# Latent attention: the next two heads' query and key products placed between the attention units of the present pair, values first

## The chip, the cores and the metric

The kernel runs on one core of a Trainium2 chip. The metric is the time of one execution on the device in microseconds; the time before is the median of three runs. One execution was also recorded by the hardware profiler, and all rows below come from it.

## What is computed

The program is a stack of two transformer models of width 1024 on 512 tokens, all in fp32. The change touches one step of the second model, the latent attention (16 heads, query and key of 64 + 32 components, values of 64). Cut to what matters:

```python
def _mla_mixer(h, w_in, q_norm, w_uq, kv_norm, w_ukv, w_out):
    cq, ckv, k_rope = jnp.split(h @ w_in, [MLA_Q_RANK, MLA_Q_RANK + MLA_KV_RANK], axis=-1)
    q = (_rmsnorm(cq, q_norm) @ w_uq).reshape(B, S, H, MLA_NOPE + MLA_ROPE)
    kv = (_rmsnorm(ckv, kv_norm) @ w_ukv).reshape(B, S, H, MLA_NOPE + MLA_V)
    q = jnp.concatenate([q[..., :MLA_NOPE], _apply_rope(q[..., MLA_NOPE:], cos, sin)], axis=-1)
    k_rope = jnp.broadcast_to(_apply_rope(k_rope[:, :, None, :], cos, sin), (B, S, H, MLA_ROPE))
    k = jnp.concatenate([kv[..., :MLA_NOPE], k_rope], axis=-1)
    v = kv[..., MLA_NOPE:]
    o = _dense_causal_attention(q * (MLA_NOPE + MLA_ROPE) ** -0.5, k, v)
    return o @ w_out
```

The causal attention takes a softmax over the keys up to each query. The ranks are 384 for the queries and 256 for keys and values.

## The kernel before

Activations lie with features on the partitions and the 512 tokens along the free axis, as blocks of 128 x 512. Each engine has its own program, in order; they meet through semaphores. TensorE's products go in turn into four PSUM banks (`pbank`, counter `m`), its small results (scores, transposes, rope turns, attention outputs) in turn into four others (`sbank`, counter `s`). `product()` and `small()` on TensorE wait until the result four places earlier in the same sequence was taken out; `full`/`sfull` wait for a result, `took`/`stook` say that its bank is free. The table `STAGES` (lines 69 to 74 for this step) fixes how many products, small results and weight blocks each stage has. The sync engine streams the weights through a ring of three tiles of 16 blocks of 128 x 128 (`stream()`, line 589 issues the loads); a tile is loaded again once TensorE has gone past it.

An fp32 product of 512 columns is two MATMUL rows of the trace. The stages of the latent attention are:

- `mla_in` (line 1022): six input products, ScalarE's copies and squares, VectorE's reciprocals (line 2072) and normed blocks (line 2075; `mla_normed` counts five, three for the queries, then two for keys and values), the rope of the one shared key part (lines 2080 to 2083), which GpSimd then copies to all 16 heads in one instruction (line 684).
- `mla_q` (line 1034): for each of 16 heads three weight blocks by 512 tokens, and one product later the rope turn, a product with the constant `turn_mla` into a small bank. ScalarE copies the query from its bank, VectorE updates the rope rows in three operations (lines 2090, 2091, 2093).
- `mla_k` (line 1043): eight key weight pairs, two heads each, two matmuls of 64 rows a head.
- `mla_v` (line 1052): values with tokens on the partitions, eight banks of results, copied by VectorE (line 2099).
- `mla` (line 1055): 64 units, `u = 4 * head + n`, where unit n of a head has 128 queries and (n + 1) x 128 keys. TensorE computes the scores of unit u; VectorE scales and masks them (line 2108), reduces the maximum (line 2111) and negates it (line 2112); ScalarE takes the exponential and its sum; VectorE takes the reciprocal (line 2118) and normalises (line 2119), one unit later. TensorE transposes the probabilities three units later (line 1074), ScalarE copies them to the area `B`, and after the fourth unit of a head TensorE forms the output product from all four. VectorE's order is score work of u, then normalisation of u - 1; ScalarE's is exponential of u, then copy of the transposes of u - 2. The order of the small results is written out in `MLA_ORDER`.
- `mla_out`: eight output products, added to the residual by VectorE.

Of the kernel before, what the change touches and what calls it, by code (L numbers as in the profile page):

```python
# [31 lines left out]
def stage(name, products, smalls, blocks):  # L32
    STAGES.append((name, products, smalls, blocks))
# [33 lines left out]
second_ffn(6)  # L67
stage("norm7", 0, 0, 0)
stage("mla_in", 6, 3, 6 * DB)
stage("mla_q", 16, 16, 3 * 16)  # L70
stage("mla_k", 16, 0, 16)
stage("mla_v", 8, 0, 16)
stage("mla", 0, 16 * 9, 0)
stage("mla_out", DB, 0, DB * DB)
second_ffn(8)
second_ffn(9)
# [42 lines left out]
def stream():  # L119


    tiles, place, skipped, plain = [], {}, 0, None
    for name, _, _, blocks in STAGES:
        w, n = AT[name][2], int("".join(c for c in name if c.isdigit()) or -1)
        if name == f"up{n}" and n in QUARTERED:
            for p in range(QUARTERED[n]):
                tiles.append(((name, p), [(0, TILE, w + skipped + TILE * p)]))
            plain = None
        elif name == f"down{n}" and n in QUARTERED:
            ff = QUARTERED[n]  # L130
            for q in range(DB // 2):
                for c, (k, nk) in enumerate(chunks(ff)):
                    tiles.append(((name, len(chunks(ff)) * q + c),
                                  [(8 * e, nk, w + skipped + (2 * q + e) * ff + k) for e in range(2)]))
            plain = None
        else:
            order = range(blocks)
            if name == "rw_in":
                order = [b for first, n_blocks in RW_PARTS.values() for b in range(first, first + n_blocks)]
            for b in order:  # L140
                if plain is None or plain == TILE:
                    tiles.append((None, []))
                    plain = 0
                place[w + b] = (len(tiles) - 1, plain)
                at, of = w + b + skipped, tiles[-1][1]
                if name in ("up1", "down1", "up4", "down4"):
                    i = b + (2 * FF1 * DB if name.startswith("down") else 0)
                    at = AT[f"up{n}"][2] + skipped + 48 * (i // 24) + i % 24
                if of and of[-1][2] + of[-1][1] == at:
                    of[-1] = (of[-1][0], of[-1][1] + 1, of[-1][2])  # L150
                else:
                    of.append((plain, 1, at))
                plain += 1
            if name in ("down1", "down4"):
                skipped += FFN_BLOCKS
    return tiles, place
# [124 lines left out]
def build(nc, io):  # L281
    with ExitStack() as ctx:
# [167 lines left out]

        MLA_ORDER = {}
        MLAG = 3
        for u in range(16 * NB + MLAG):
            if u < 16 * NB:
                MLA_ORDER["scores", u] = len(MLA_ORDER)
            if u >= MLAG:
                MLA_ORDER["turned", u - MLAG] = len(MLA_ORDER)
                if (u - MLAG) % NB == NB - 1:
                    MLA_ORDER["output", (u - MLAG) // NB] = len(MLA_ORDER)

        def mla_small(what, u):
            return AT["mla"][1] + MLA_ORDER[what, u]
# [255 lines left out]
        def _(pe):  # L718
# [312 lines left out]
            s = small()  # L1031
            done(pe, AT["mla_in"][0] + 5)
            mm(sbank(s)[:, :], const("turn_mla"), B[:, 21, :], True, True, small_full)
            begin("mla_q")
            for j in range(17):
                if j < 16:
                    project(lambda k: B[:, 16 + k, :], 3,
                            (lambda k: pe.wait_ge(S("mla_normed"), k + 1)) if j == 0 else settled, cols=96)
                if j >= 1:
                    s = small()  # L1040
                    done(pe, AT["mla_q"][0] + j - 1)
                    mm(sbank(s)[0:96, :], const("turn_mla")[0:96, 0:96], A[0:96, j - 1, :], True, True, small_full)
            begin("mla_k")
            pe.wait_ge(S("mla_normed"), 5)
            for j in range(8):
                w = weight(2)
                for e in range(2):
                    m = product()
                    for k in range(2):
                        mm(pbank(m)[0:64, :], w[:, k * P + 64 * e:k * P + 64 * e + 64], B[:, 19 + k, :], k == 0, k == 1,  # L1050
                           product_full if k == 1 else None)
            begin("mla_v")
            for half in range(2):
                token_major(lambda k: B[:, 19 + k, :], 2, T, settled)
            begin("mla")
            pe.wait_ge(S("mla_q_ready"), 16)
            pe.wait_ge(S("mla_keys_spread"), 1)
            for j in range(4):
                done(pe, AT["mla_k"][0] + 12 + j)
            for j in range(4):  # L1060
                done(pe, AT["mla_v"][0] + 4 + j)
            for u in range(16 * NB + MLAG):
                if u < 16 * NB:
                    hd, n = u // NB, u % NB
                    s = small()
                    mm(sbank(s)[:, 0:(n + 1) * P], A[0:96, hd, n * P:(n + 1) * P], B[0:96, hd, 0:(n + 1) * P], True, True,
                       small_full)
                if u >= MLAG:
                    v = u - MLAG
                    hd, n = v // NB, v % NB  # L1070
# [5 lines left out]
                    if n == NB - 1:  # L1076
                        o = small()
                        for j in range(NB):
                            sdone(pe, mla_small("turned", v - 3 + j))
                        rows = slice(64 * (hd % 2), 64 * (hd % 2) + 64)  # L1080
                        for b in range(NB):
                            mm(sbank(o)[rows, b * P:], A[:, 16 + 2 * b + hd // 8, hd % 8 * 64:hd % 8 * 64 + 64],
                               B[:, 16 + 4 * (hd % 2) + b, b * P:], b == 0, b == NB - 1,
                               small_full if b == NB - 1 else None)
            begin("mla_out")
            sdone(pe, mla_small("output", 14))
            sdone(pe, mla_small("output", 15))
# [239 lines left out]
        def _(act):  # L1327
# [210 lines left out]
            for j, width in ((0, 384), (1, 256)):  # L1538
                sfull(act, s0 + j)
                stook(a(TM[:, j, :], sbank(s0 + j)[:, :], ACT.Sqrt, scale=1 / width, bias=vec("eps", 0)), s0 + j)  # L1540
            m0 = AT["mla_q"][0]
            for j in range(16):
                full(act, m0 + j)
                took(a(A[0:96, j, :], pbank(m0 + j)[0:96, :], ACT.Identity), m0 + j)
            m0 = AT["mla_k"][0]
            for j in range(16):
                full(act, m0 + j)
                took(a(B[0:64, j, :], pbank(m0 + j)[0:64, :], ACT.Identity), m0 + j)
            for u in range(16 * NB + MLAG - 1):
                if u < 16 * NB:  # L1550
                    n, o = u % NB, u % 4
                    act.wait_ge(S("mla_minus_max"), u + 1)
                    p = TM[:, o, 0:(n + 1) * P]
                    a(p, p, ACT.Exp, bias=SM[:, o:o + 1], accum_out=SM[:, 4 + o:5 + o]).then_inc(S("mla_exp"), 1)
                if u < MLAG - 1:
                    continue
                v = u - MLAG + 1
# [2 lines left out]
                sfull(act, s)  # L1560
                if v >= 8 and n == 0:
                    sfull(act, mla_small("output", hd - 2))
                stook(a(B[:, 16 + 4 * (hd % 2):17 + 4 * (hd % 2) + n, n * P:(n + 1) * P],
                        sbank(s)[:, 0:(n + 1) * P].rearrange("p (b t) -> p b t", t=P), ACT.Identity), s)
                if n == NB - 1:
                    s = mla_small("output", hd)
# [123 lines left out]
        def _(dve):  # L1690
# [390 lines left out]
            own(tt(kr, kr, cos, ALU.mult))  # L2081
            sdone(dve, s0 + 2)
            tt(kr, kr, TM[64:96, 2, :], ALU.add).then_inc(S("mla_key"), 1)
            s0 = AT["mla_q"][1]
            for j in range(16):
                q, t = A[64:96, j, :], TM[64:96, 2 + j % 2, :]
                sfull(dve, s0 + j)
                if j == 0:
                    dve.wait_ge(S("mla_key"), 1)
                stook(tt(t, sbank(s0 + j)[64:96, :], sin, ALU.mult), s0 + j)  # L2090
                own(tt(q, q, cos, ALU.mult))
                sdone(dve, s0 + j)
                tt(q, q, t, ALU.add).then_inc(S("mla_q_ready"), 1)
            m0 = AT["mla_v"][0]
            for half in range(2):
                for t in range(NB):
                    m = m0 + 4 * half + t
                    full(dve, m)
                    took(dve.tensor_copy(A[:, 16 + 2 * t + half, :], pbank(m)[:, :]), m)
            scale = float(96 ** -0.5)  # L2100
            for u in range(16 * NB + 1):
                if u < 16 * NB:
# [10 lines left out]
                if u >= 1:  # L2113
# [3 lines left out]
                    dve.wait_ge(S("mla_exp"), v + 1)  # L2117
                    own(dve.reciprocal(SM[:, 8 + o:9 + o], SM[:, 4 + o:5 + o]))
                    ts(w, w, SM[:, 8 + o:9 + o], None, ALU.mult).then_inc(S("mla_probs"), 1)
            add_gated("mla_out", 1)  # L2120
            norm2(8, 2)
            up_silu(8)
# [352 lines left out]
```

## Time and profile before

| what | value |
|---|---|
| median of three runs | 4630.73 us (4629.33 to 4631.75) |
| the profiled execution | 4628.95 us, span 4627.1 us |
| TensorE busy | 4311.6 us, 93% |
| VectorE, ScalarE, GpSimd busy | 34%, 14%, 36% |
| TensorE's mean granted clock | 0.956 of full speed |
| the attention units, 2523 to 2693.3 us | 170 us |

A busy share is the time in which an engine executed instructions over the span; a TensorE that is busy may still run at half of its clock. Times in the timeline are microseconds from the span's start, then the duration; in square brackets stands the idle time before an instruction and what ended it.

### The profile page before, as it was taken

How to read it: one execution, taken by the hardware profiler on the slowest of the kernel's cores; microseconds unless marked ns; L12 is line 12 of the kernel's file. 1: busy time of each engine (PE TensorE's matmuls, PEld its weight loads, DVE VectorE, ACT ScalarE, POOL GpSimd, SP SyncE). 2: the span in 40 equal slices, each digit the busy share in tenths (PEclk: the TensorE clock that was granted, in tenths of full speed). 3: DMA queues.
4: the chain of work that ended last, by engine and by line, in shares of the span. 5: the costliest groups of instructions: out<-in, count | busy, mean ns of one | idle time of the engine just before them, and what ended most of it. 6: DMA issues, size and time to landing. Idle time of an engine off the chain costs nothing.

```text
span 4627.1 us, 40198 instructions
## 1 busy us (share of the span) xinstructions
PE 4311.6 (93%) x15784; PEld 2713.2 (59%) x15784; DVE 1581.5 (34%) x2889; ACT 663.2 (14%) x1407; POOL 1663.6 (36%) x1520
## 2 busy tenths in 40 slices
PE   7948999999999999899999789999999889989998
PEld 3323444433644444388853338887888336836887
DVE  3062111026721110333225533323331754453432
ACT  1131000012610000100012410001000231211000
POOL 0003888800048886044410004443443015003442
PEclk9969999999899999999999889999999889989999
DMA  3102434311034342122221012222222123112222
GB/s 120 64 0 109 154 141 155 114 70 55 10 132 155 141 154 104 55 85 89 84 67 45 0 46 86 88 85 74 88 87 86 46 84 92 36 37 73 82 87 68
DMA packets 124346, 387.39 MB, mean 84 GB/s; under 512 B 37568, under 2 KB 40640, under 8 KB 110080
## 3 DMA queue, kind: packets, MB, share of 16 engines
q1 hardware_dynamic: 108848, 302.56, 19.5%
q0 software_dynamic: 15312, 82.27, 4.7%
q8 instruction: 126, 2.06, 0.2%
q14 instruction: 60, 0.49, 0.0%
HBM read 376.39 MB, written 8.39 MB: 83 GB/s over the span
## 4 chain that ended last, share of the span: by engine, by line
PE 89%; DVE 7%; ACT 2%; issue 1%; DMA 1%; POOL 0%; DVEq 0%; ACTq 0%; POOLq 0%
PE bank L722 89%; DVE rstd L1711 1%; DVE normed L1713 1%; ACT temporary L1331 1%; DVE temporary L2323 1%; DVE small_columns L2111 1%; DVE temporary L2108 0%; DMA constant_matrices<-in_constants_dram 0%; ACT area_b L1331 0%; ACT L1331 0%; PE bank L993 0%; DVE normed L1716 0%; DVE temporary L1855 0%; DVE area_b L1818 0%; ACT squares L1331 0%
## 5 line engine op out<-in xcount | busy, mean ns | idle before, releaser
L722 PE MATMUL bank<-normed,weight_ring 128*128 128x512 f32 (+2 forms) x4080 | 1514.1, 528 | 77.0 <-DVE normed L1716 36.1
L722 PEld LDWEIGHTS bank<-normed,weight_ring 128*128 128x128 f32 (+1 forms) x4080 | 781.5, 193 | 766.3 <-issue 689.9
L722 PE MATMUL bank<-area_a,weight_ring 128*128 128x512 f32 (+1 forms) x1776 | 634.9, 514 | 15.3 <-issue 15.3
L722 PEld LDWEIGHTS bank<-area_a,weight_ring 128*128 128x128 f32 x1776 | 339.2, 192 | 288.1 <-issue 267.6
L672 POOL TENSOR_TENSOR area_b<-weight_ring 128x512 f32<-128x512 f32 (+1 forms) x68 | 84.1, 1236 | 1171.7 <-issue 563.1
L722 PE MATMUL bank<-area_b,weight_ring 128*128 128x256 f32 (+3 forms) x1616 | 497.3, 455 | 5.9 <-issue 2.8
L642 POOL TENSOR_SCALAR area_b<-area_b,small_columns 128x384 f32<-128x384 f32 x336 | 418.9, 1247 | 0.0
L722 PEld LDWEIGHTS bank<-area_b,weight_ring 128*128 128x128 f32 (+2 forms) x1616 | 302.2, 187 | 176.7 <-issue 145.4
L644 POOL TENSOR_TENSOR area_b<-area_b 128x384 f32<-128x384 f32 x336 | 335.4, 998 | 28.0
L722 PE MATMUL bank<-area_b 128*128 128x256 f32 (+2 forms) x1200 | 259.7, 379 | 16.2 <-ACT area_d L1331 16.2
L722 PEld LDWEIGHTS bank<-area_b 128*128 128x128 f32 (+1 forms) x1200 | 215.8, 197 | 51.9 <-ACT area_d L1331 16.9
L672 POOL TENSOR_TENSOR area_d<-weight_ring 128x512 f32<-128x512 f32 (+1 forms) x68 | 84.1, 1236 | 449.8 <-PE bank L722 424.4
L722 PE MATMUL bank<-area_b,area_d 128*128 128x256 f32 x1056 | 239.0, 379 | 0.0
L722 PEld LDWEIGHTS bank<-area_b,area_d 128*128 128x128 f32 x1056 | 200.6, 190 | 27.3
L722 PE MATMUL bank<-squares,constant_matrices 128*128 128x512 f32 x282 | 146.1, 645 | 68.4 <-ACT squares L1331 46.2
L722 PE MATMUL bank<-area_b,area_a 128*64 128x128 f32 (+11 forms) x640 | 166.9, 414 | 40.0 <-ACT area_b L1331 22.9
L722 PE MATMUL bank<-normed,area_d 128*128 128x256 f32 (+2 forms) x1088 | 197.9, 339 | 0.2 <-issue 0.2
L1331 ACT ACTIVATE area_d<-area_d 128x512 f32<-128x512 f32 (+1 forms) x104 | 57.7, 563 | 920.9 <-DVE area_d L2012 920.9
L2032 DVE SCALAR_TENSOR_TENSOR residual<-temporary,modulations,residual 128x256 f32<-128x256 f32 x64 | 41.4, 646 | 379.3 <-ACT temporary L1331 378.1
L722 PEld LDWEIGHTS bank<-normed,area_d 128*128 128x128 f32 (+2 forms) x1088 | 156.3, 171 | 24.4 <-issue 2.9
L1331 ACT ACTIVATE temporary<-bank 128x256 f32<-128x256 f32 (+1 forms) x136 | 58.9, 433 | 774.1 <-PE bank L722 774.1
L1746 DVE TENSOR_TENSOR residual<-residual,bank 128x512 f32<-128x512 f32 x32 | 22.0, 688 | 428.6 <-PE bank L722 428.6
(267 smaller groups left out, 4500.7 us busy)
## 6 DMA issues: line engine op xcount, KB each, us to landing
weight_ring<-in_weights_dram SPq DMA_DIRECT2D x377, 512.0 KB, 4.6
weight_ring<-in_weights_dram SPq DMA_DIRECT2D x61, 1024.0 KB, 4.8
area_b<-in_weights_dram POOLq DMA_DIRECT2D x48, 1024.0 KB, 5.2
area_b<-in_weights_dram POOLq DMA_DIRECT2D x48, 512.0 KB, 6.4
weight_ring<-in_weights_dram SPq DMA_DIRECT2D x40, 384.0 KB, 4.4
weight_ring<-in_weights_dram SPq DMA_DIRECT2D x24, 256.0 KB, 3.7
low_scratch<-area_d SPq DMA_DIRECT2D x16, 256.0 KB, 2.0
area_d<-low_scratch SPq DMA_DIRECT2D x16, 256.0 KB, 2.8
```

What stands on the lines that cost most here:

```text
L642: po.tensor_scalar(scaled, part, c, None, ALU.mult).then_inc(S("pool_step"), 1)
L644: i = po.tensor_tensor(total, total, scaled, ALU.add)
L672: po.tensor_tensor(s1, w21, w22, ALU.add).then_inc(S("pool_sum"), 1)
L722: i = pe.matmul(out, lhsT, rhs, start=start, stop=stop)
L1331: return act.activation(out, in_, func, **kw)
L1711: own(dve.reciprocal(RB[:, :], RB[:, :]))
L1713: i = stt(H[:, k, :], X[:, k, :], gain(k), RB[:, :], ALU.mult, ALU.mult)
L1746: took(tt(X[:, k, :], X[:, k, :], pbank(m0 + k)[:, :], ALU.add), m0 + k)
L2032: return stt(x, part, g, x, ALU.mult, ALU.add)
L2111: own(dve.tensor_reduce(SM[:, o:o + 1], w, AX, ALU.max))
L2323: own(dve.reciprocal(r, r))
```

## The change

The stages `mla_q` and `mla_k` are gone. Values come first. Queries, keys and rope turns of heads 0 and 1 follow, and those of each later pair stand between the units of the pair before it: on TensorE the two queries behind the scores of the first two units of a pair, the keys of both behind the third, the two rope turns behind the fifth and sixth. Scores of a head wait for its own query and key. ScalarE takes queries and keys between exponential and transposed copy; VectorE does the rope updates at the ends of its sixth and seventh unit of a pair. The transposed probabilities lie in the area `D` in place of `B`, the rope's scratch in `D` in place of `TM`. The weight blocks are streamed in the new order. The diff, cut:

```diff
-stage("mla_q", 16, 16, 3 * 16)
-stage("mla_k", 16, 0, 16)
-stage("mla_v", 8, 0, 16)
-stage("mla", 0, 16 * 9, 0)
+stage("mla_v", 8, 0, 0)
+stage("mla", 32, 16 * 10, 3 * 16 + 16 + 16)
...
+            if name == "mla":
+
+                order = [*range(64, 80)]
+                for pair in range(8):
+                    order += [*range(6 * pair, 6 * pair + 6), 48 + 2 * pair, 49 + 2 * pair]
...
+        for hd in range(2):
+            MLA_ORDER["rope", hd] = len(MLA_ORDER)
         for u in range(16 * NB + MLAG):
             if u < 16 * NB:
                 MLA_ORDER["scores", u] = len(MLA_ORDER)
+            if u < 14 * NB and u % 8 in (4, 5):
+                MLA_ORDER["rope", u // 8 * 2 + u % 8 - 2] = len(MLA_ORDER)
             if u >= MLAG:
                 MLA_ORDER["turned", u - MLAG] = len(MLA_ORDER)
...
+            def query(hd):
+                at["w"] = w0 + 3 * hd
+                project(lambda k: B[:, 16 + k, :], 3, settled, cols=96)
+
+            def keys(pair):
+                at["w"] = w0 + 48 + 2 * pair
                 w = weight(2)
                 for e in range(2):
                     m = product()
                     for k in range(2):
                         mm(pbank(m)[0:64, :], w[:, k * P + 64 * e:k * P + 64 * e + 64], B[:, 19 + k, :], k == 0, k == 1,
                            product_full if k == 1 else None)
+
+            def rope(hd):
+                s = small()
+                done(pe, mla_query(hd))
+                mm(sbank(s)[0:96, :], const("turn_mla")[0:96, 0:96], A[0:96, hd, :], True, True, small_full)
+
             begin("mla_v")
+            at["w"] = w0 + 64
             for half in range(2):
-                token_major(lambda k: B[:, 19 + k, :], 2, T, settled)
+                token_major(lambda k: B[:, 19 + k, :], 2, T, lambda k: pe.wait_ge(S("mla_normed"), 5) if k == 0 else None)
+            at["w"] = w0
             begin("mla")
-            pe.wait_ge(S("mla_q_ready"), 16)
+            query(0)
+            query(1)
+            keys(0)
+            rope(0)
+            rope(1)
             pe.wait_ge(S("mla_keys_spread"), 1)
...
                     s = small()
+                    if n == 0:
+                        pe.wait_ge(S("mla_q_ready"), hd + 1)
+                        done(pe, mla_key(hd))
                     mm(sbank(s)[:, 0:(n + 1) * P], A[0:96, hd, n * P:(n + 1) * P], B[0:96, hd, 0:(n + 1) * P], True, True,
                        small_full)
+                if u < 14 * NB:
+                    if u % 8 in (0, 1):
+                        query(u // 8 * 2 + 2 + u % 8)
+                    elif u % 8 == 2:
+                        keys(u // 8 + 1)
+                    elif u % 8 in (4, 5):
+                        rope(u // 8 * 2 + u % 8 - 2)
...
                     a(p, p, ACT.Exp, bias=SM[:, o:o + 1], accum_out=SM[:, 4 + o:5 + o]).then_inc(S("mla_exp"), 1)
+                if u < 14 * NB:
+                    hd = u // 8 * 2 + 2
+                    if u % 8 in (1, 2):
+                        query(hd + u % 8 - 1)
+                    elif u % 8 in (3, 4):
+                        key(hd + u % 8 - 3)
...
+            def rope(hd):
+                q, t, s = A[64:96, hd, :], D[64:96, 8 + hd % 2, :], mla_small("rope", hd)
+                sfull(dve, s)
+                stook(tt(t, sbank(s)[64:96, :], sin, ALU.mult), s)
                 own(tt(q, q, cos, ALU.mult))
-                sdone(dve, s0 + j)
+                sdone(dve, s)
                 tt(q, q, t, ALU.add).then_inc(S("mla_q_ready"), 1)
...
+            dve.wait_ge(S("mla_key"), 1)
+            rope(0)
+            rope(1)
...
                     ts(w, w, SM[:, 8 + o:9 + o], None, ALU.mult).then_inc(S("mla_probs"), 1)
+                if u < 14 * NB and u % 8 in (5, 6):
+                    rope(u // 8 * 2 + u % 8 - 3)
```

## Rows read from the trace of the kernel before

**Rows 1.** The page: busy time of each engine, and the chain that ended last

```profile
PE 4311.6 (93%) x15784; PEld 2713.2 (59%) x15784; DVE 1581.5 (34%) x2889; ACT 663.2 (14%) x1407; POOL 1663.6 (36%) x1520
...
PE 89%; DVE 7%; ACT 2%; issue 1%; DMA 1%; POOL 0%; DVEq 0%; ACTq 0%; POOLq 0%
```

**Rows 2.** Busy time by stage, the attention: length; PE, PEld, DVE, ACT, POOL; clock; DMA share; GB/s

```profile
2523.00:2693.30 170.30, 124.94 (x417) 58.40 (x417) 98.16 (x322) 72.93 (x208) 0.00 (x0) 0.85 0.00 1
```

**Rows 3.** The chain of waits ahead of the attention: start, length, what

```profile
2423.65 2.81 issue
2426.46 96.89 PE bank L722 x224
```

**Rows 4.** Timeline of TensorE at the first score and over one head, with ScalarE's last copy

```profile
2524.31 2.40 PE L722 MATMUL bank<-area_b,area_a 96*128 96x128 f32 x8 [0.98 <-DVE area_a L2099]
...
2578.27 3.39 PE L722 MATMUL bank<-area_b,area_a 128*64 128x512 f32 x10 [1.46 <-ACT area_b L1331]
2581.50 0.27 PE L1074 MATMUL bank<-constant_matrices,temporary 128*128 128x128 f32 x1
...
2582.45 0.70 PE L722 MATMUL bank<-area_b,area_a 96*128 96x256 f32 x2 [0.23 <-DVE temporary L2108]
2583.98 0.52 PE L1074 MATMUL bank<-constant_matrices,temporary 128*128 128x128 f32 x3 [0.83 <-DVE temporary L2119]
...
2585.28 0.63 PE L1074 MATMUL bank<-constant_matrices,temporary 128*128 128x128 f32 x4
2587.36 3.39 PE L722 MATMUL bank<-area_b,area_a 128*64 128x512 f32 x10 [1.46 <-ACT area_b L1331]
...
2586.64 0.58 ACT L1331 ACTIVATE area_b<-bank 128x512 f32<-128x512 f32 x1
```

**Rows 5.** Timeline of VectorE: a rope update, and the masked scores

```profile
2442.69 0.68 DVE L2090 TENSOR_TENSOR temporary<-bank,area_b 32x512 f32<-32x512 f32 x1
...
2444.61 0.68 DVE L2090 TENSOR_TENSOR temporary<-bank,area_b 32x512 f32<-32x512 f32 x1
...
2528.59 0.68 DVE L2108 SCALAR_TENSOR_TENSOR temporary<-bank,constant_matrices 128x512 f32<-128x512 f32 x1
...
2581.70 0.69 DVE L2108 SCALAR_TENSOR_TENSOR temporary<-bank,constant_matrices 128x512 f32<-128x512 f32 x1 [2.60 <-PE bank L722]
...
2586.41 0.55 DVE L2108 SCALAR_TENSOR_TENSOR temporary<-bank,constant_matrices 128x384 f32<-128x384 f32 x1
...
2587.84 0.35 DVE L2119 TENSOR_SCALAR temporary<-temporary,small_columns 128x256 f32<-128x256 f32 x1
2590.80 0.69 DVE L2108 SCALAR_TENSOR_TENSOR temporary<-bank,constant_matrices 128x512 f32<-128x512 f32 x1 [2.60 <-PE bank L722]
...
2684.10 0.69 DVE L2108 SCALAR_TENSOR_TENSOR temporary<-bank,constant_matrices 128x512 f32<-128x512 f32 x1 [2.60 <-PE bank L722]
```

**Rows 6.** Timeline around the normed blocks and the copy of the rope key

```profile
2430.98 1.41 DVE L2075 SCALAR_TENSOR_TENSOR area_b<-area_b,vector_columns,temporary 128x512 f32<-128x512 f32 x2
...
2434.50 7.00 POOL L684 COPY area_b<-area_b 32x8192 f32<-32x8192 f32 x1 [73.48 <-DVE area_b L2083]
2434.54 0.69 DVE L2090 TENSOR_TENSOR temporary<-bank,area_b 32x512 f32<-32x512 f32 x1
...
2435.15 6.90 DVE L2091 TENSOR_TENSOR area_a<-area_a,area_b 32x512 f32<-32x512 f32 x1
```

**Rows 7.** TensorE's restart before `mla_in`, and busy time by stretch (columns of rows 2)

```profile
2372.92 12.46 PE L722 MATMUL bank<-normed,weight_ring 128*128 128x512 f32 x23 [5.62 <-issue]
...
2370.50:2377.50 7.00, 4.58 (x6) 1.97 (x7) 6.79 (x12) 0.00 (x0) 0.00 (x0) 0.52 0.00 0
...
2545.26:2548.30 3.04, 3.04 (x5) 0.96 (x6) 0.76 (x4) 0.00 (x0) 0.00 (x0) 0.50 0.00 0
...
2565.40:2566.30 0.90, 0.01 (x1) 0.04 (x1) 0.87 (x3) 0.75 (x3) 0.00 (x0) 0.50 0.00 0
2566.30:2572.10 5.80, 5.80 (x10) 2.37 (x11) 0.76 (x4) 1.24 (x3) 0.00 (x0) 0.50 0.00 1
```

More of the change, by code:

```diff
@@ L459, in build, with mla_query, mla_key @@
                     MLA_ORDER["output", (u - MLAG) // NB] = len(MLA_ORDER)
+        def mla_query(hd):
+            return AT["mla"][0] + 4 * (hd // 2) + hd % 2
+        def mla_key(hd):
+            return mla_query(hd) + 2
         def mla_small(what, u):
@@ L1033, in _ @@
             mm(sbank(s)[:, :], const("turn_mla"), B[:, 21, :], True, True, small_full)
[L1034 to L1045, printed above, removed]
+            w0 = AT["mla"][2]
+            def query(hd):
[3 more added lines that the diff above has]
+                at["w"] = w0 + 48 + 2 * pair
                 w = weight(2)
@@ L1051, in _ @@
                            product_full if k == 1 else None)
+            def rope(hd):
+                s = small()
+                done(pe, mla_query(hd))
+                mm(sbank(s)[0:96, :], const("turn_mla")[0:96, 0:96], A[0:96, hd, :], True, True, small_full)
             begin("mla_v")
+            at["w"] = w0 + 64
             for half in range(2):
-                token_major(lambda k: B[:, 19 + k, :], 2, T, settled)
+                token_major(lambda k: B[:, 19 + k, :], 2, T, lambda k: pe.wait_ge(S("mla_normed"), 5) if k == 0 else None)
+            at["w"] = w0
             begin("mla")
-            pe.wait_ge(S("mla_q_ready"), 16)
+            query(0)
[3 more added lines that the diff above has]
+            rope(1)
             pe.wait_ge(S("mla_keys_spread"), 1)
-            for j in range(4):
-                done(pe, AT["mla_k"][0] + 12 + j)
             for j in range(4):
@@ L1082, in _ @@
                             mm(sbank(o)[rows, b * P:], A[:, 16 + 2 * b + hd // 8, hd % 8 * 64:hd % 8 * 64 + 64],
-                               B[:, 16 + 4 * (hd % 2) + b, b * P:], b == 0, b == NB - 1,
+                               D[:, 4 * (hd % 2) + b, b * P:], b == 0, b == NB - 1,
                                small_full if b == NB - 1 else None)
+            at["w"] = AT["mla_out"][2]
             begin("mla_out")
@@ L1540, in _, with query, key @@
                 stook(a(TM[:, j, :], sbank(s0 + j)[:, :], ACT.Sqrt, scale=1 / width, bias=vec("eps", 0)), s0 + j)
[L1541 to L1548, printed above, removed]
+            def query(hd):
+                m = mla_query(hd)
+                full(act, m)
+                took(a(A[0:96, hd, :], pbank(m)[0:96, :], ACT.Identity), m)
+            def key(hd):
+                m = mla_key(hd)
+                full(act, m)
+                took(a(B[0:64, hd, :], pbank(m)[0:64, :], ACT.Identity), m)
+            for hd in range(2):
+                query(hd)
+            for hd in range(2):
+                key(hd)
             for u in range(16 * NB + MLAG - 1):
@@ L1562, in _ @@
                     sfull(act, mla_small("output", hd - 2))
-                stook(a(B[:, 16 + 4 * (hd % 2):17 + 4 * (hd % 2) + n, n * P:(n + 1) * P],
+                stook(a(D[:, 4 * (hd % 2):1 + 4 * (hd % 2) + n, n * P:(n + 1) * P],
                         sbank(s)[:, 0:(n + 1) * P].rearrange("p (b t) -> p b t", t=P), ACT.Identity), s)
@@ L2083, in _ @@
             tt(kr, kr, TM[64:96, 2, :], ALU.add).then_inc(S("mla_key"), 1)
[L2084 to L2090, printed above, removed]
+            def rope(hd):
+                q, t, s = A[64:96, hd, :], D[64:96, 8 + hd % 2, :], mla_small("rope", hd)
+                sfull(dve, s)
+                stook(tt(t, sbank(s)[64:96, :], sin, ALU.mult), s)
                 own(tt(q, q, cos, ALU.mult))
-                sdone(dve, s0 + j)
+                sdone(dve, s)
                 tt(q, q, t, ALU.add).then_inc(S("mla_q_ready"), 1)
```

## Prediction

> **What bounds the kernel now.** I read the page first [rows 1]: one core, TensorE busy for 93% of the span, and the chain that ended last runs over its matmuls for 89%. A change pays only where TensorE waits or runs at its lower clock. Next the table by stage [rows 2]: in the 170 us of the latent attention TensorE is busy for 124.9 and its granted clock is 0.85, that is, part of the time at 1.2 instead of 2.4 GHz. Just before it the chain of waits [rows 3] has 224 product matmuls in 96.9 us with no gap: queries, keys, values. So there is a full stretch ahead of a stretch with holes, and the change pours the one into the other.
>
> How large are the holes? The timeline of one head [rows 4] with its VectorE side [rows 5] gives it. From one masked score of 512 columns (2581.70) to the next (2590.80) are 9.1 us, at full clock. TensorE's own work in them is 3.23 us for the output product and the last score (2578.27 to 2581.50), 1.3 for the 768 columns of the other scores at the pace of the products, and 1.1 for ten transposes: 5.6. The 16 such rows run from 2528.59 to 2684.10, 155.5 us for 15 intervals, five of them of 9.1 and the others of 10.4 to 12.0. 15 x 9.1 is 136.5, and the other **19.0 us are the clock** [rows 5, 7].
>
> About 0.2% (9.3 us) is what a measurement of this kernel can tell from no change.
>
> **Part 1, the work taken out ahead.** Of the 224 matmuls (0.4325 us each [rows 3]) 16 x 12 belong to queries, keys and rope turns, 32 to the values. The 12 of each of 14 heads move: 168 x 0.4325 = **-72.7 us** there. No matmul is added or dropped, and no DMA: the same 80 weight blocks in another order, used more slowly, with the ring filled ahead as now. I cost that at nothing; the products that no longer run back to back are its cover.
>
> **Part 2, values first.** Queries need only the first normed block, and TensorE started on them at 2426.46 [rows 3]. Values need the fifth, which ends at 2430.98 + 1.41 = 2432.39 [rows 6], and about 0.1 more to start: **+6.1 us**. The idle time becomes 2.8 + 6.1 = 8.9 us. After the 5.6 us hole before the stage's first products TensorE restarted at 2372.92 and the clock stood at 0.52 until 2377.5 [rows 7]: 4.6 us at half clock, 2.3 lost. I take **+2.3** for the values; the ends are 0 and 3.4 (half of the longest slow stretch, 6.8 us).
>
> GpSimd's copy of the rope key runs from 2434.50 for 7.00 us. VectorE's rope multiplication that began beside it took 6.90 us instead of 0.67, while the one at 2434.54, with an operand in PSUM, took 0.69 [rows 6]. Now the value copies from PSUM lie there. I cost them at nothing. If they were held to 2441.5, the fifth value product, due after 16 matmuls (2432.5 + 6.9 + 2.3 = 2441.7), would wait for a bank until about 2442.3: +0.6, or +2.9 without the slow clock. The Trainium skill (SBUF — State Buffer, "Who interferes with whom") says that a VectorE instruction with two SBUF inputs is locked out by a reading GpSimd instruction and one with at most one SBUF input, outside the two-port modes, is not; by it the sum would stay as it is.
>
> **Part 3, start of the attention.** Two rope updates stand before the first score. A rope update is three VectorE operations, 1.92 us from one head to the next (2442.69 to 2444.61 [rows 5]). The first ends some 2.2 us after its turn matmul (1.99 and the signals), of which the second turn covers 0.9; TensorE waits 1.4 us where it now waits 1.0 for the last value copy: **+0.5**.
>
> **Part 4, units with queries or keys** (the first three units of a pair). Two queries of 6 matmuls and a key pair of 8: 20 x 0.4325 = 8.65 us per pair. They stand between a score and the transpose three units back, and TensorE is in order. Laid end to end, one interval is 5.6 + 8.65 us, and one wait stays: the last transpose of a head comes only behind the keys, and from its start to the output product are 0.63 for it, 0.58 for ScalarE's copy [rows 4] and 0.17 for signals, of which TensorE works 0.43 and waits 0.95. That gives 15.2 instead of 9.1: **6 x 6.1 = +36.6**. For the first pair the same 8.65 lie between the first and the fourth score; that stretch was 4.3 us (2524.31 to 2528.59) and becomes the sum of its matmuls, 10.8 + 0.2: **+6.8**.
>
> **Part 5, units with rope turns** (fifth and sixth of a pair, seven times). Here lies the catch. Small results share four banks in order of issue: score 44, turn 12, transpose 41, score 45, turn 13, transpose 42, score 46, transpose 43, output 10. So transpose 42 takes the bank of turn 12, and output 10 that of turn 13. VectorE empties turn 12 only after the normalisation of unit 44. From the 512-column score to that point VectorE has 4.7 us of work without a pause (2581.70 to 2586.41 [rows 5]); add 0.69 for the rope's first operation and 0.1 for the signal, and transpose 42 starts 5.6 us after it, where it now starts 2.3 after (2583.98 [rows 4]). Behind it in TensorE's queue stands score 46: 0.3 for the transposes, 0.9 until VectorE has it, 1.43 for its mask, reduction, sign and the reciprocal of unit 45 (2586.41 to 2587.84), 0.27 for that unit's normalisation, and only then the second rope operation, 0.8 with its signal. These 3.7 us later output 10 starts, 9.3 after the 512-column score instead of 5.7 (2587.36). The interval becomes 12.8 for 9.1: **7 x 3.7 = +25.7**, to carry turns that cost 1.7 us each time.
>
> At full clock: 6.1 + 0.5 - 72.7 + 36.6 + 6.8 + 25.7 = **+3.0 us**. The overlap gives back only 0.6 us a pair, which the late start eats.
>
> **Part 6, the clock.** Now the clock falls in ten of 15 intervals, each time near the end of the thin part of a head. In one, 3.04 us of the output product ran slow, 1.5 lost; in another the clock fell earlier, 0.9 us ahead of it (2565.4), and 5.8 ran slow, 2.9 lost [rows 7]. After the change the query and key intervals have no wait over 1 us, so I cost no fall there. In the rope intervals about 2.3 us of matmuls lie in the 7.7 us ahead of the output, thinner than now (1.8 in 4.9, from 2582.45 on), so a fall comes each time and mostly earlier. The ends of its price are 0 and 3.4; I take 2.6, near the later of the two rows, as the wait ahead of the output is longer than in either: 7 x 2.6 = 18.2. The last two intervals stay as they are, 2 x 1.27 (19.0 / 15) = 2.5. So 20.7 in place of 19.0: **+1.7**, beside the 2.3 of part 2.
>
> **Sum:** 3.0 + 2.3 + 1.7 = +7.0 us. The profiled execution took 4628.95 (span 4627.1 and 1.85 around it) and would take 4636.0; it lies 1.8 below the median of the runs, so against 4630.73 the forecast is 4637.7, +0.15%, which counts as no change.
>
> **Rivals.**
> A, full clock. TensorE is busier in the stage (77% of a pair by my layout, 62% now at full clock), and if that holds the clock at 2.4 GHz in all seven rope intervals and the last two, 18.2 + 2.5 go, and 2.3 with them: 4637.7 - 23.0 = 4614.7. For it: the whole product stretch ran at 1.00. Against it: the falls of now follow thin moments, not thin stages. The Trainium skill (TensorE: Matmul & The Clock Gate, "What's actually happening") lets the clock follow how busy the array has recently been; that alone leaves open which of the two decides. Chance 0.09.
> B, no bank wait. If the transposes did not stand behind the turns' banks, the rope intervals would stay at 9.1 and fall as now: 4637.7 - 25.7 - 7 x 1.33 = 4602.7. The order of small results in the code speaks against it. Chance 0.05.
> C, slower. The half clock begins so far ahead of the even outputs that it holds on through the queries behind them, 3.4 us each time: 7 x 0.8 = +5.6 over my value, 4643.3. It decides from 2.93 a fall. The 5.8 us row is for it; against it, intervals of 12.0 us are only three of the ten long ones now. Chance 0.22, and 0.1 more for waits that I have not seen on that side.
> My forecast: 0.54.
>
> The range leaves out most of A and B and takes in C with 3.4 at the values and the held copies, rounded: 4622 to 4647. Faster by over 0.2% is A and B, 0.14; slower is C and the unseen waits, 0.32; the rest, 0.54, within.
>
> **What would show it.** First value matmul near 2432.5 at half clock. The 512-column masked scores at distances that alternate near 15.2 and 15.4 (12.8 and the fall). TensorE's waits before a transpose and an output product, released by VectorE's rope line, 2.2 and 2.3 us, seven each. Granted clock 1.00 in query intervals, half once a pair. I am wrong if the two intervals sum to under 27 us (clock or bank wait missing) or over 32, or if the value copies lengthen past 0.69.

## The result, and the profile after the change

The changed kernel takes 4640.12 us, the median of 17 runs (4639.23 to 4642.59); the kernel before, measured beside it, 4630.48 (17 runs, 4628.79 to 4632.40). The ratio is 1.0021 with a 95% interval of 1.0014 to 1.0029: +9.6 us where +7.0 was forecast. The change makes the kernel slightly slower. The prediction called anything up to 9.3 us no change; the measured difference lies 0.3 us beyond that line, and its interval (+6.5 to +13.4 us) covers both sides of it. The profiled execution took 4641.61 us. From its page:

```profile
span 4639.8 us, 40225 instructions
...
PE 4313.5 (93%) x15784; PEld 2715.6 (59%) x15784; DVE 1578.8 (34%) x2889; ACT 661.0 (14%) x1407; POOL 1664.1 (36%) x1520
```

The same 15784 matmuls, as in [rows 1]. All of this execution lies 2.46 us later from before the stage on (VectorE's reciprocal for the queries starts at 2424.68, before at 2422.22), which the code does not explain: it is the same up to there. In the profiled executions of the other runs below this instruction starts between 2422.21 and 2425.26, so such an offset belongs to the execution. So the query start of [rows 3], 2426.46, answers to 2428.92 here. From there to the first product of `mla_out` were 266.85 us (2426.46 to 2693.31) and are 276.56 (to 2705.48): **+9.7 us in the stage**, and what follows takes 1934.3 us where it took 1933.8. TensorE's timeline, with the start of the stage, one query interval and one rope interval:

```profile
2434.92 15.59 PE L735 MATMUL bank<-weight_ring,area_b 128*128 128x512 f32 x32 [8.80 <-DVE area_b L2117]
2450.34 8.89 PE L735 MATMUL bank<-area_b,weight_ring 128*96 128x512 f32 x20
...
2462.63 0.46 PE L735 MATMUL bank<-area_b,area_a 96*128 96x128 f32 x2 [1.50 <-DVE area_a L2132]
...
2497.23 3.65 PE L735 MATMUL bank<-area_b,weight_ring 128*64 128x512 f32 x8
2500.81 0.66 PE L1103 MATMUL bank<-constant_matrices,temporary 128*128 128x128 f32 x4
2502.24 2.34 PE L735 MATMUL bank<-area_d,area_a 128*64 128x512 f32 x8 [0.78 <-ACT area_d L1361]
...
2508.06 1.10 PE L735 MATMUL bank<-area_a,constant_matrices 96*96 96x512 f32 x2 [0.57 <-DVE temporary L2151]
2511.25 0.55 PE L1103 MATMUL bank<-constant_matrices,temporary 128*128 128x128 f32 x3 [2.09 <-DVE area_d L2129]
2511.63 0.81 PE L735 MATMUL bank<-area_b,area_a 96*128 96x384 f32 x2
2512.28 0.60 PE L1103 MATMUL bank<-constant_matrices,temporary 128*128 128x128 f32 x4
2515.11 4.53 PE L735 MATMUL bank<-area_d,area_a 128*64 128x512 f32 x8 [2.23 <-DVE area_d L2129]
```

The hole of 8.80 us ahead of the values is there. In the rope interval a transpose and the output product wait 2.09 and 2.23 us, and the releaser is line 2129, the first operation of the rope update: the one that frees the turn's bank. The chain of waits in total (engine and tile, waited for what, us, times, longest) says the same of all seven:

```profile
PE bank L735 <- DVE area_d L2129: 15.1, 7, 2.2
PE bank L1103 <- DVE area_d L2129: 14.6, 7, 2.1
```

The masked 512-column scores of VectorE, the first, those around one rope and one query interval with the two rope updates between, and the last; they answer to [rows 5]:

```profile
2473.99 0.69 DVE L2151 SCALAR_TENSOR_TENSOR temporary<-bank,constant_matrices 128x512 f32<-128x512 f32 x1 [2.84 <-PE bank L735]
...
2505.68 0.69 DVE L2151 SCALAR_TENSOR_TENSOR temporary<-bank,constant_matrices 128x512 f32<-128x512 f32 x1 [6.55 <-PE bank L735]
...
2510.50 0.69 DVE L2129 TENSOR_TENSOR area_d<-bank,area_b 32x512 f32<-32x512 f32 x1
...
2514.36 0.69 DVE L2129 TENSOR_TENSOR area_d<-bank,area_b 32x512 f32<-32x512 f32 x1
...
2520.96 0.69 DVE L2151 SCALAR_TENSOR_TENSOR temporary<-bank,constant_matrices 128x512 f32<-128x512 f32 x1 [4.60 <-PE bank L735]
...
2536.42 0.69 DVE L2151 SCALAR_TENSOR_TENSOR temporary<-bank,constant_matrices 128x512 f32<-128x512 f32 x1 [6.55 <-PE bank L735]
...
2696.00 0.69 DVE L2151 SCALAR_TENSOR_TENSOR temporary<-bank,constant_matrices 128x512 f32<-128x512 f32 x1 [4.15 <-PE bank L735]
```

A rope interval is 15.28 us (2505.68 to 2520.96), a query interval 15.46. The clock, by stretch (length; PE, PEld, DVE, ACT, POOL busy; clock; DMA share; GB/s):

```profile
2508.10:2513.10 5.00, 2.69 (x11) 1.28 (x11) 4.72 (x13) 2.80 (x10) 0.00 (x0) 1.00 0.00 0
2513.10:2515.10 2.00, 0.00 (x0) 0.00 (x0) 1.87 (x6) 0.41 (x1) 0.00 (x0) 0.54 0.01 4
2515.10:2520.10 5.00, 4.99 (x9) 2.17 (x10) 1.23 (x2) 0.43 (x1) 0.00 (x0) 0.50 0.00 0
2520.10:2536.40 16.30, 15.52 (x50) 6.54 (x49) 6.26 (x20) 5.68 (x16) 0.00 (x0) 1.00 0.00 0
```

It fell about 2.0 us ahead of the output product, inside the second wait; 5.0 us of matmuls ran at 1.2 GHz (2.5 lost), and the query interval after it is at 1.00. So in six of the seven pairs. In the first pair the clock fell earlier, inside the first wait (at 2479.1), and stayed down to 2489.4, over the transposes and the next score too; that rope interval is 16.23 us.

### The profile page after: what moved, and what is told of

The parts are those of the page before. It is cut to its first block, busy times and chain, and to the rows that moved or that the text cites. A ratio compares the mean times of both kernels' runs of the same rounds, so it can differ in the third digit from the quotient of the medians.

```text
span 4639.8 us, 40225 instructions
## 1 busy us (share of the span) xinstructions
PE 4313.5 (93%) x15784; PEld 2715.6 (59%) x15784; DVE 1578.8 (34%) x2889; ACT 661.0 (14%) x1407; POOL 1664.1 (36%) x1520
## 4 chain that ended last, share of the span: by engine, by line
PE 89%; DVE 7%; ACT 2%; issue 1%; DMA 0%; POOL 0%; DVEq 0%; ACTq 0%; POOLq 0%
PE bank L735 89%; DVE rstd L1753 1%; DVE normed L1755 1%; DVE temporary L2368 1%; ACT temporary L1361 0%; DMA constant_matrices<-in_constants_dram 0%; DVE temporary L2151 0%; DVE small_columns L2154 0%; ACT L1361 0%; PE bank L1006 0%; DVE normed L1758 0%; DVE temporary L1897 0%; ACT squares L1361 0%; DVE area_b L1860 0%; PE bank L1103 0%
## 5 line engine op out<-in xcount | busy, mean ns | idle before, releaser
L735 PE MATMUL bank<-area_a,weight_ring 128*128 128x512 f32 (+1 forms) x1776 | 635.1, 514 | 15.3 <-issue 15.3
L735 PE MATMUL bank<-normed,area_b 128*128 128x256 f32 x704 | 166.3, 379 | 0.0
```

The source lines that it names most:

```text
L735: i = pe.matmul(out, lhsT, rhs, start=start, stop=stop)
```

## The experiments

The theory is the one of the prediction: the late start, the crowd of products in one interval, the banks held by the rope turns in the other, and the half clock that the resulting holes bring on. The intervals below are distances of the 512-column masked scores on VectorE, unless TensorE is named. The diffs are cut to the lines that carry the idea.

**Values first, alone, on the kernel before.** The values become the first stage of products, the rest stays in whole stages:

```diff
-stage("mla_q", 16, 16, 3 * 16)
-stage("mla_k", 16, 0, 16)
 stage("mla_v", 8, 0, 16)
+stage("mla_q", 16, 16, 3 * 16)
+stage("mla_k", 16, 0, 16)
```

> The kernel before with one part of the change alone: values ahead of queries and keys, which stay whole stages. Theory: 6.0 us for the later start and 1.6 us of slow clock at the values, 7.6 us more than before, 4638. The value copies beside GpSimd's copy keep 0.69 us. Rival (the start is hidden behind something later): 4630.5. Rival (GpSimd's copy holds the value copies up to its end): up to 3 us more than the theory.

Measured: 4637.91 us (11 runs) beside 4630.86, ratio 1.0015 (1.0006 to 1.0024), +7.1 us. TensorE's timeline:

```profile
2434.40 15.59 PE L722 MATMUL bank<-weight_ring,area_b 128*128 128x512 f32 x32 [8.81 <-DVE area_b L2074]
2449.82 5.31 PE L722 MATMUL bank<-area_b,weight_ring 128*96 128x512 f32 x12
```

The hole is 6.0 us longer than the 2.81 of [rows 3], and the 32 value matmuls take 15.42 us from start to start where 32 x 0.4325 is 13.8: 1.6 lost to the clock. The eight value copies took 0.69 us each, also the first four (2440.58 to 2443.85), which ran beside GpSimd's copy (2436.45 to 2443.45), so nothing was held. The start costs 7.6 us by its rows, 7.1 by the median. Over the whole stage this execution is 6.5 us longer than the one before: in the attention units the clock happened to cost 1.4 us less (154.1 us for 155.5).

**Values first undone, on the changed kernel.**

```diff
+            begin("mla_first")
+            query(0, lambda k: pe.wait_ge(S("mla_normed"), k + 1))
+            query(1)
+            pe.wait_ge(S("mla_normed"), 5)
+            keys(0)
             begin("mla_v")
...
             begin("mla")
-            query(0)
-            query(1)
-            keys(0)
             rope(0)
```

> The changed kernel with one part undone: the queries and keys of heads 0 and 1 stand ahead of the values again. My theory prices values first at the 6.0 us by which TensorE started later and 1.6 us of slow clock at the values. Queries can start at the first normed block, 5.2 us of them fill all but 0.8 us of the gap, and the values start at full clock: 6.8 us less than the changed kernel, about 4633. Rival (the late start is hidden, since VectorE's rope of the first heads sets the start of the attention): no change, 4640.

Measured: 4634.61 us (11 runs), 5.5 less than the changed kernel for 6.8 expected; against the kernel before the ratio is 1.0008 (0.9999 to 1.0017), which leaves open whether the rest of the change costs anything in total. The timeline:

```profile
2427.93 5.36 PE L736 MATMUL bank<-area_b,weight_ring 128*96 128x512 f32 x12 [2.81 <-issue]
2433.92 3.65 PE L736 MATMUL bank<-area_b,weight_ring 128*64 128x512 f32 x8 [0.63 <-DVE area_b L2121]
2437.50 14.00 PE L736 MATMUL bank<-weight_ring,area_b 128*128 128x512 f32 x32
...
2454.72 0.46 PE L736 MATMUL bank<-area_b,area_a 96*128 96x128 f32 x2 [1.51 <-DVE area_a L2136]
```

The queries fill all but 0.63 us of the gap and the values run at full clock. From the first query to the first score are 26.8 us, where the changed kernel needs 33.7 from the same point: 6.9 less, as expected. The rest of the intervals stayed at 15.3 and 15.45. Both runs agree: this part is about 7 of the 10 us in the stage. The interleaving that is left has no gain to set against it; from the query start to the first product of `mla_out` it takes 269.7 us in this trace, 2.9 more than the kernel before.

**Rope turns in the product banks.** Only the banks change, not the order of any engine; VectorE reads the turn from its new bank:

```diff
             def rope(hd):
-                s = small()
+                m = product()
                 done(pe, mla_query(hd))
-                mm(sbank(s)[0:96, :], const("turn_mla")[0:96, 0:96], A[0:96, hd, :], True, True, small_full)
+                mm(pbank(m)[0:96, :], const("turn_mla")[0:96, 0:96], A[0:96, hd, :], True, True, product_full)
```

> The changed kernel with the rope turns written to the four product banks, so that no transpose or output product takes a bank that VectorE empties late; VectorE's order and all else stay. Theory (the bank order holds TensorE for 2.1 and 2.2 us in each rope interval, and these holes let the clock fall): the rope intervals go from 15.3 to about 10.3 us, where VectorE's own work with two rope updates ends, the query intervals from 15.45 to about 14 since their keys no longer meet a late score, the falls nearly vanish: about 41 us less, 4599. Rival (it is VectorE's time for the two rope updates that delays the output, whatever the bank): rope intervals stay over 14 us and the time over 4630.

Measured: 4600.91 us (4 runs), ratio to the kernel before 0.9935 (0.9921 to 0.9948), 39.2 less than the changed kernel. The rope intervals are 10.72 us and the query intervals 13.83. TensorE in one rope interval, with its 512-column scores at both ends and the one after the next query interval, and VectorE's masked scores at the ends of the rope interval:

```profile
2522.27 1.13 PE L734 MATMUL bank<-area_b,area_a 96*128 96x512 f32 x2
...
2525.08 1.02 PE L734 MATMUL bank<-area_a,constant_matrices 96*96 96x512 f32 x2
2525.94 0.49 PE L1102 MATMUL bank<-constant_matrices,temporary 128*128 128x128 f32 x3
2526.27 0.81 PE L734 MATMUL bank<-area_b,area_a 96*128 96x384 f32 x2
2527.01 0.63 PE L1102 MATMUL bank<-constant_matrices,temporary 128*128 128x128 f32 x4
2529.10 2.34 PE L734 MATMUL bank<-area_d,area_a 128*64 128x512 f32 x8 [1.47 <-ACT area_d L1360]
2531.37 1.12 PE L734 MATMUL bank<-area_b,area_a 96*128 96x512 f32 x2
...
2546.83 1.12 PE L734 MATMUL bank<-area_b,area_a 96*128 96x512 f32 x2
```

```profile
2523.44 0.69 DVE L2150 SCALAR_TENSOR_TENSOR temporary<-bank,constant_matrices 128x512 f32<-128x512 f32 x1 [6.54 <-PE bank L734]
...
2534.16 0.69 DVE L2150 SCALAR_TENSOR_TENSOR temporary<-bank,constant_matrices 128x512 f32<-128x512 f32 x1
```

Transpose and output product no longer wait for line 2129's counterpart. On TensorE the rope interval, from one 512-column score to the next, is 9.10 us (2522.27 to 2531.37), what it was without turns at full clock, and the query interval 15.46 (to 2546.83), as in the changed kernel. VectorE with its two rope updates reaches the second score 1.6 us late (no idle time before 2534.16) and makes that up in the query interval; this is why its own distances read 10.72 and 13.83. It does not set the pace, as had been expected. From 2500 to 2630 the granted clock is 1.00; in the last two intervals it still falls (0.74 from 2630 to 2670). The rival (VectorE's time, whatever the bank) falls: it is the bank.

**Fillers in the two waits of the changed kernel.** The results are never read; the computation is otherwise complete.

```diff
+            def filler(n):
+                m = at["m"]
+                pe.wait_ge(product_done[m % 4], m // 4)
+                for _ in range(n):
+                    pe.matmul(pbank(m)[:, :], const("ident"), C[:, CAT["causal"]:CAT["causal"] + T], start=True, stop=True)
...
                         rope(u // 8 * 2 + u % 8 - 2)
+                        if u % 8 == 5:
+                            filler(2)
...
+                        if u < 14 * NB and u % 8 == 6:
+                            filler(2)
                         o = small()
```

> The changed kernel with two matmuls of 512 columns (1.7 us at full clock) more in each of the two waits of a rope interval, their results never read; the waits are 2.1 and 2.2 us, so at full clock they cost nothing. Theory (2.5 us of each rope interval are half clock, because TensorE is too idle ahead of the output product): the clock stays at 1.00 in all seven, the intervals go from 15.3 to 12.8, 17 us less, 4623. Rival (the 2.5 us are waits of another kind, or the filler does not hold the clock): no change or slower, 4640 to 4650.

Measured: 4620.28 us (9 runs), ratio 0.9976 (0.9967 to 0.9985), 19.8 less than the changed kernel, by adding 28 fp32 matmuls. TensorE's timeline of one rope interval, then the busy time by stretch:

```profile
2503.17 1.88 PE L1072 MATMUL bank<-constant_matrices 128*128 128x512 f32 x4
2505.42 0.55 PE L1112 MATMUL bank<-constant_matrices,temporary 128*128 128x128 f32 x3 [0.37 <-DVE area_d L2140]
...
2506.89 1.88 PE L1072 MATMUL bank<-constant_matrices 128*128 128x512 f32 x4
2509.28 2.37 PE L735 MATMUL bank<-area_d,area_a 128*64 128x512 f32 x8 [0.50 <-DVE area_d L2140]
```

```profile
2500.00:2650.00 150.00, 137.93 (x447) 60.70 (x445) 89.61 (x253) 60.55 (x165) 0.00 (x0) 1.00 0.04 15
```

The waits are still there, filled; the releaser is the same; the output product takes 2.37 us for 4.53. The seven rope intervals are 12.89 us each, the 12.8 laid out at full clock, and the query intervals stay at 15.45. That separates the parts: of the 6.2 us by which a rope interval (15.3) exceeds 9.1, 3.8 are the wait for the banks (12.9) and 2.4 the clock; in the first pair the clock's part is 3.3. The last two intervals fell to 9.1 too (from 10.8 and 10.6) with no filler in them; so falls there come and go, and what decides is not shown; of the 20.9 us by which the 15 intervals became shorter, 3.2 are that.

**One filler in the kernel before.** The same `filler(1)` ahead of each output product.

> The kernel before with one more matmul of 512 columns (0.86 us, result never read) in the wait of 1.46 us ahead of each output product of the attention. Theory (19.0 us of the 15 intervals, and 1.4 at the last output, are half clock that thin activity brings on): the intervals become 9.1 us throughout, 19 to 20 us less than before, 4611. Rival (the clock follows something else than what TensorE does just ahead of the output): 4630, or more where the filler runs at half clock.

Measured: 4609.08 us (5 runs) beside 4631.44, ratio 0.9953 (0.9940 to 0.9965), 22.4 us less.

```profile
2581.39 0.63 PE L1081 MATMUL bank<-constant_matrices,temporary 128*128 128x128 f32 x4
2581.86 1.02 PE L1057 MATMUL bank<-constant_matrices 128*128 128x512 f32 x2
2583.48 3.39 PE L722 MATMUL bank<-area_b,area_a 128*64 128x512 f32 x10 [0.60 <-ACT area_b L1339]
```

The wait of 1.46 us in [rows 4] is 0.60 behind the filler. Fourteen of 15 intervals are 9.09 or 9.10 us, the first 9.8, and from 2540 to 2668 the clock is 1.00. Of the 19.0 us that the prediction gave to the clock, 18.4 are gone (155.5 us became 137.1). From the query start to `mla_out` the trace is 18.7 us shorter and behind it 1.7; the other 2.0 of the 22.4 are between the two medians and these two executions.

**The same work spread evenly.** One query behind a head's first score, one key and one turn in the wait ahead of the output product, in each of the first 14 heads, for the head two later; VectorE's rope update at the end of the third unit.

```diff
-                if u < 14 * NB:
-                    if u % 8 in (0, 1):
-                        query(u // 8 * 2 + 2 + u % 8)
-                    elif u % 8 == 2:
-                        keys(u // 8 + 1)
-                    elif u % 8 in (4, 5):
-                        rope(u // 8 * 2 + u % 8 - 2)
+                if u < 14 * NB and u % NB == 0:
+                    query(u // NB + 2)
...
                     i.then_inc(small_full, 1)
+                if u < 14 * NB and u % NB == 2:
+                    key(u // NB + 2)
+                    rope(u // NB + 2)
+                if u >= MLAG:
                     if n == NB - 1:
                         o = small()
```

> The changed kernel with the same work spread evenly: one query behind the first score of every head, one key and one rope turn behind the last transpose of the head before, that is, in the wait ahead of the output product; VectorE's rope update at the end of the third unit. Theory (the change loses because 8.65 us of products crowd one interval, in front of the transposes, and the turns hold banks in the other): every interval near TensorE's own work, 10.8 us instead of 15.4, no falls of the clock, 14 x 4.6 = 64 us less than the changed kernel, about 4575. Rival (TensorE's work per head plus the waits of the softmax chain adds up wherever it is put): 9.1 + 5.15 = 14.2 us an interval, about 4623.

Measured: 4583.19 us (4 runs), ratio 0.9896 (0.9882 to 0.9909): 48.2 less than the kernel before, 56.9 less than the changed one. One head on TensorE:

```profile
2563.88 1.93 PE L736 MATMUL bank<-area_b,weight_ring 128*64 128x512 f32 x4
2565.74 1.10 PE L736 MATMUL bank<-area_a,constant_matrices 96*96 96x512 f32 x2
2566.77 2.37 PE L736 MATMUL bank<-area_d,area_a 128*64 128x512 f32 x8
2569.07 1.13 PE L736 MATMUL bank<-area_b,area_a 96*128 96x512 f32 x2
...
2577.99 2.37 PE L736 MATMUL bank<-area_d,area_a 128*64 128x512 f32 x8
```

No row in the head has an idle time; 11.22 us from output to output is TensorE's own work. Expected was 10.8, so the layout was 0.4 short; the trace doesn't split that between the 5.6 us counted for a head's own scores, transposes and output and the 5.2 for the rest. Over 14 heads it is 6 of the 8 us by which the time missed the expected 4575. The turns are in the small banks again, yet nothing waits for them: VectorE reads the turn of 2565.74 at 2566.88, before its bank comes round. This order undoes the crowd and the bank wait at once. Of its 56.9 us, moving the banks alone brought 39.2: a pair of heads takes TensorE 30.7 us in the changed kernel, 24.6 with other banks, 22.4 here.

**Spread, with queries first.** Both edits together.

> The spread order together with queries and keys of heads 0 and 1 ahead of the values. Theory: the 6.8 us of the start add to the spread order's gain, about 4568. Rival (with no slow clock left the start matters less, or the start is hidden): the same as the spread order alone.

Measured: 4575.92 us (4 runs), ratio 0.9880 (0.9865 to 0.9895): 7.3 less than the spread order alone, as the start is worth elsewhere (7.6 by its rows). Run again unchanged, beside the next one:

> The same kernel as e7, unchanged, beside e8 for a comparison on the same chip: 4576 again, 4.5 us above e8.

it took 4575.87.

**And a filler for the last heads,** which have no later products beside them: `filler(1)` ahead of the output products from unit 56 on.

> The spread order with queries and keys of heads 0 and 1 first, and one filler matmul of 512 columns ahead of the output products of the last heads, which have no products of later heads beside them. In the run without it the last two intervals were 10.8 and 10.5 us and the clock fell three times. Theory (half clock from thin activity there): intervals of 9.1 us and the last output product 1.4 us shorter, 4.5 us less than the 4575.9 without filler, about 4571. Rival (the ends are bound by waits): 4576.

Measured: 4567.84 us (4 runs), ratio 0.9864 (0.9849 to 0.9878), 8.0 less than without. The end of the stage without (the first of the two runs) and with the filler:

```profile
2634.67 4.03 PE L737 MATMUL bank<-area_d,area_a 128*64 128x512 f32 x8 [0.78 <-ACT area_d L1365]
2639.43 25.99 PE L737 MATMUL bank<-normed,weight_ring 128*128 128x512 f32 x60 [0.73 <-issue]
```

```profile
2631.68 2.37 PE L737 MATMUL bank<-area_d,area_a 128*64 128x512 f32 x8
2634.77 30.71 PE L737 MATMUL bank<-normed,weight_ring 128*128 128x512 f32 x71 [0.73 <-issue]
```

The last two intervals are 9.1 us for 10.8 and 10.5, and the stage ends 4.7 us earlier (with starts that differ by 0.1), as expected. Another 2.0 us lie after the stage (1934.2 and 1932.2 us from `mla_out` to the end). The trace shows where half of them go: behind the next norm TensorE restarts after the same idle 5.66 us, and its next 40 matmuls take 16.1 us where they took 17.1; counted from the start of `mla_out`, the clock fell 2 us earlier and was back 2 us earlier. The filler in the kernel before did the same (1932.1 for 1933.8 us after the stage). The rest is open.

## Why the prediction was right, point by point

The mechanisms came out as laid; the sum was 2.7 us short (9.7 in the stage for 7.0). By the prediction's own line between no change and slower (9.3 us) the outcome falls just on the slower side, through several small terms and not through rival C.

- **Part 1.** The 168 matmuls left the stretch ahead; no matmul more or less.
- **Part 2.** Later start 6.0 us for 6.1. The slow clock cost 1.6 for 2.3. The held copies did not come; GpSimd's copy took 7.00 us again and the value copies beside it 0.69 each. With the rule of the Trainium skill (SBUF — State Buffer, "Who interferes with whom") that a VectorE instruction with at most one SBUF input, outside the two-port modes, is not locked out, the trace agrees: these copies read PSUM alone, and the four beside GpSimd's copy took 0.69 us like the four after it.
- **Part 3 and 4, the start.** From the last value matmul to the first score 12.3 us (2450.34 to 2462.63) for 11.8 in my terms (24 matmuls and 1.4); the wait itself was 1.50 for 1.4. From there to the first 512-column score 11.36 for 11.1.
- **Part 4, query intervals.** 15.46 for 15.2, six times: +1.5 us. The term that was too small is TensorE's own work: in a query interval it is busy for 14.68 us (2520.96 to 2536.42) where 5.6 and 8.65 were counted, and the spread order shows 11.22 us of unbroken work where 5.6 and 5.2 were. The wait before the output was rather overstated: 0.78 us for 0.95.
- **Part 5, rope intervals.** Transpose 5.57 us after the masked score (2505.68 to 2511.25) for 5.6, output product 9.43 for 9.3. Full-clock length 12.89 in the run with fillers for 12.8. The bank order was the cause of the 3.7 us: with other banks TensorE's rope interval is 9.10, so the turns themselves cost nothing there.
- **Part 6, the clock.** One fall a pair, each ahead of the output product, 2.4 us for 2.6 in six pairs and 3.3 in the first; none began in a query interval. The seven rope intervals make 107.9 us in sum for 107.8, which is in part luck: 0.6 us more at full clock and 0.7 more in the first pair stand against 1.3 less in the six other falls. The last two intervals and the end took 1.0 us more than counted.
- **Rivals.** A (full clock) fell: the clock went down in all seven rope intervals and the last two, though the stage as a whole became denser. B (no bank wait) fell for the changed kernel. The run with other banks is the kernel that B described, and its 4600.9 us lie near B's 4602.7; but B had the clock fall there (7 x 1.33) and it did not, so that closeness is in part luck. C asked for over 2.93 us a fall; they were 2.4 but for the first pair's 3.3. The mechanism of the forecast case held, and its time ended 0.3 us past its upper edge, by the small errors above, which mostly have one sign.

## What to carry to other kernels

Work moved from a dense stretch into a stretch with holes is free only where it lands in the holes: put it behind the last thing that the critical chain needs and ahead of the wait, a piece per period, not a crowd in one period. Whatever shares a rotating set of banks must be emptied in the order and at the pace of its neighbours, or one late reader holds results that have nothing to do with it. And a product that waits briefly at the same place each period may also run at half clock behind the wait, as here after waits of 1.46 and 2.2 us; a look at the granted clock there tells.

## What the runs showed that was not expected

- Matmuls that do nothing make the kernel faster. 16 in the kernel before, 14 of them inside a wait of 1.46 us, the first and the last in one of 0.78, bring 22.4 us (0.5%): the granted clock stays at 2.4 GHz in 14 of 15 intervals, where it fell in ten.
- The same small hole may cost or not: the last two intervals took 10.8 and 10.6 us in the changed kernel and 9.1 and 9.1 in the one whose fillers stood only in earlier heads.
- The interleaving that the change aimed at is worth 56 us (1.2%) once it is spread and the queries come first, 63.6 us with the filler (ratio 0.9864), while its first form loses 9.6.
